# Fourteen more low-part units of a two-block transformer kernel move from VectorE to GpSimd

## The reference, cut to what matters

```python
h    = rmsnorm(x, pre_norm_mix) * (1 + scale_m) + shift_m
q_lat, kv_lat, k_idx, w_idx, z, xbc, dt_raw, g_a, g_b = split(h @ w_in)
qn    = rmsnorm(q_lat, q_norm)
q     = qn @ w_uq                      # 16 heads x 128
q_idx = qn @ w_qidx                    # 16 index heads x 64
rel    = relu(einsum('bqhd,bsd->bqhs', q_idx, k_idx))
iscore = einsum('bqh,bqhs->bqs', w_idx * scale, rel)      # sum over the index heads
iscore = where(key_chunk <= query_chunk, iscore, -inf)
_, idx = top_k(iscore, 64)
logits = q . kv[idx] * scale + bias(position distance);   probs = softmax(logits)
o      = (probs . kv[idx]) @ w_uv @ w_o_attn
y_b    = ssd_mixer(z, xbc, dt_raw, ...) @ w_o_ssd
```

## Time and profile before

| | us |
|---|---|
| median of three executions | 973.84 |
| the profiled execution's own time | 973.98 |
| its span | 972.0 |
| PE busy | 946.3 (97%) |
| DVE busy | 669.4 (69%) |
| ACT busy | 544.4 (56%) |
| POOL busy | 242.2 (25%) |

### The profile page before, as it was taken

The page is one execution under the profiler, slowest core; times in us unless marked ns, Lnnn a source line. Parts: engine busy times, 40 slices in busy tenths (PEclk is TensorE's granted clock), DMA queues, the critical chain, the costliest instruction groups (busy, mean ns, idle before and its releaser), DMA issues.

```text
span 972.0 us, 16471 instructions
## 1 busy us (share of the span) xinstructions
PE 946.3 (97%) x6121; PEld 829.3 (85%) x6121; DVE 669.4 (69%) x1094; ACT 544.4 (56%) x956; POOL 242.2 (25%) x239
## 2 busy tenths in 40 slices
PE   9999999999999999999999999999999999999997
PEld 8987777888877798899989999998889778888786
DVE  5765567777785668975668666677985767755453
ACT  6667666444443666834547455557863754544443
POOL 5205002111122231299932143330230021000100
PEclk9999999999999999999999999999999999999999
DMA  9755347789987713760139756653246677656561
GB/s 293 217 161 190 94 147 231 229 276 289 284 274 257 247 51 97 208 174 22 34 102 311 236 165 183 172 144 88 75 147 213 219 237 242 211 175 192 194 221 66
DMA packets 141594, 179.04 MB, mean 184 GB/s; under 512 B 8124, under 2 KB 117390, under 8 KB 141520
## 3 DMA queue, kind: packets, MB, share of 16 engines
q1 hardware_dynamic: 130624, 144.53, 47.6%
q0 software_dynamic: 10304, 33.18, 11.5%
q10 hardware_dynamic: 592, 0.34, 0.1%
HBM read 176.90 MB, written 1.12 MB: 183 GB/s over the span
## 4 chain that ended last, share of the span: by engine, by line
PE 80%; DVE 8%; ACT 6%; DMA 3%; issue 2%; SPq 0%; DVEq 0%; ACTq 0%
PE bank L1932 26%; PE bank L2021 12%; PE bank L2023 11%; PE bank L2022 11%; DVE w_lo L1333 3%; ACT w_hi L869 2%; PE bank L2191 1%; PE bank L2454 1%; PE bank L1963 1%; PE bank L2450 1%; PE bank L2477 1%; DMA w_raw<-in_w_in 1%; PE bank L2385 1%; PE bank L2073 1%; DMA w_raw<-in_w_down 1%
## 5 line engine op out<-in xcount | busy, mean ns | idle before, releaser
L1333 DVE TENSOR_TENSOR w_lo<-w_raw,w_hi 128x1024 fp32r<-128x1024 f32 (+1 forms) x239 | 286.0, 1221 | 91.2 <-ACT w_hi L869 86.8
L869 ACT ACTIVATE w_hi<-w_raw 128x1024 fp32r<-128x1024 f32 (+1 forms) x258 | 262.1, 1037 | 117.7 <-PE bank L2023 50.6
L1932 PE MATMUL bank<-h_hi,w_hi 128*128 128x256 f32 x560 | 162.9, 291 | 1.9 <-DVE w_lo L1333 1.0
L1932 PE MATMUL bank<-h_lo,w_hi 128*128 128x256 f32 x560 | 158.3, 283 | 0.0
L1932 PE MATMUL bank<-h_hi,w_lo 128*128 128x256 f32 x560 | 158.2, 282 | 0.0
L2021 PE MATMUL bank<-w_hi,h_hi 128*128 128x512 f32 x384 | 152.1, 396 | 1.9 <-DVE h_lo L1333 1.9
L2023 PE MATMUL bank<-w_hi,h_lo 128*128 128x512 f32 x384 | 150.3, 391 | 0.0
L2022 PE MATMUL bank<-w_lo,h_hi 128*128 128x512 f32 x384 | 150.1, 391 | 0.0
L1932 PEld LDWEIGHTS bank<-h_hi,w_hi 128*128 128x128 f32 x560 | 107.2, 191 | 3.4 <-DVE w_lo L1333 2.0
L1932 PEld LDWEIGHTS bank<-h_lo,w_hi 128*128 128x128 f32 x560 | 107.3, 192 | 0.0
L1932 PEld LDWEIGHTS bank<-h_hi,w_lo 128*128 128x128 f32 x560 | 107.1, 191 | 0.0
(11 more groups left out here) (463 smaller groups left out, 1810.3 us busy)
## 6 DMA issues: line engine op xcount, KB each, us to landing
w_raw<-in_w_in SPq DMA_DIRECT2D x84, 512.0 KB, 3.8
ada_raw<-in_ada_w POOLq DMA_DIRECT2D x48, 512.0 KB, 6.0
w_raw<-in_w_gate_up SPq DMA_DIRECT2D x88, 256.0 KB, 5.4
w_raw<-in_w_ffn_in SPq DMA_DIRECT2D x88, 256.0 KB, 4.0
w_raw<-in_w_down SPq DMA_DIRECT2D x22, 512.0 KB, 6.5
w_raw<-in_w_ffn_out SPq DMA_DIRECT2D x22, 512.0 KB, 4.5
w_raw<-in_w_out SPq DMA_DIRECT2D x16, 512.0 KB, 4.0
w_raw<-in_w_o_ssd SPq DMA_DIRECT2D x16, 512.0 KB, 3.4
```

What stands on the lines that cost most here:

```text
L869: act.activation(high(u, n), w_raw[:, u % RING, 0:n], ACT.Copy).then_inc(hi_ready, 1)
L1333: return dve.tensor_tensor(dst, src, hi.bitcast(F32), ALU.subtract)
L1932: ins = pe.matmul(out_b[:, s, :], w[:, kk, c], x[:, k0 + k, :], start=k == 0 and s == 0 and step == 0, stop=k == sum(st.ks) - 1 and s == 1 ...
```

## The change

POOL makes the low parts of the eight `w_uq` units, of all ten `z` units and of the first two `s_z2` units, twenty in all where it made six; it does so ahead of its wait for the index sums, of the DMA of `w_uv` and of `reached`. DVE makes none from the first `w_uq` unit to the second unit of `s_z2`: its two low parts ahead of the rounds, the one in each round, the three before the top-k and the two behind the mask go.

```diff
-    pool_topk = range(s_z.u0 + 4, s_z2.u0)
+    pool_topk = range(s_uq.u0, s_z2.u0 + 2)
...
         pool.affine_select(out=pick[:, :], in_=pick[:, :], pattern=[[-1, 16 * P]], compare_op=ALU.is_ge,
                            fill=0.0, base=15, channel_multiplier=16).then_inc(pick_ready, 1)
+        for u in range(s_uq.u0, s_z.u0):
+            split(u)
+        for u in range(s_z.u0, s_z2.u0 + 2):
+            split(u)
         pool.wait_ge(ix_sum, 8)
         pool.dma_start(w_uv[:, :, :], a["w_uv_2"].rearrange("h c d -> c h d")).then_inc(uv_in, 16)
-        for u in pool_topk:
-            split(u)
...
-        split_to(s_uq.u0 + 2)
         for r in range(8):
...
             ins.then_inc(ix_sum, 1)
-            split_to(min(s_uq.u0 + r + 3, s_z.u0 + 1))
             dve.wait_ge(ix_sum, r + 1)
         link(dve.tensor_tensor(isc[:, :, :], isc[:, :, :], shut[:, :, :], ALU.add))
-        split_to(s_z.u0 + 4)
...
         dve.tensor_tensor(mask[:, :, :], isc[:, :, :], shut[:, :, :], ALU.add).then_inc(mask_ready, 1)
-        split_to(s_z2.u0 + AHEAD)
+        split_to(s_z2.u0)
```

## The result

The changed kernel takes 979.84 us in the median (978.83 to 981.28, four runs) against 973.23 (972.25 to 973.98): the ratio is 1.0068, 95% interval 1.0056 to 1.0081. It is slower by 6.6 us where 3.8 were forecast. The direction was right; the time is 2.2 us above the forecast of 977.6 and 0.2 us above the upper end of the range, 979.6.

The account below looks back on a forecast made before the run. PE was taken to bound the kernel, so time is won only where PE stands still. Lead -1.7, wait +4.0 and clock +1.5 gave +3.8 us: 977.8 on the profiled execution, forecast 977.6 us, range 975.2 to 979.6.

Parts of the forecast that it names:

- The three holes: PE's idle waits before the first `w_uq` unit (1.15 us), z0 (0.40) and z1 (0.91): 2.46 us, all the change can win.
- the lead s: PE's lead over the old timetable from the filled holes, after held sums: taken as 1.7 us.
- The shared port: DVE operations with two SBUF inputs wait for the running POOL instruction; index sums fall behind by 0.53 us a round.
- the mask, held twice: DVE's mask behind the top-k, delayed by two POOL splits, is there by 427.6.
- the dearer port: Rival: POOL gets between the sums more often, s about 0, wait 4.0 us, with the clock +5.5: 979.3; chance 0.14.
- The queue on POOL: Two `s_z2` splits, `w_uv` DMA and `reached` end at 432.0 - s; PE waits 4.0 us before the first logits tile.
- its three signs of being wrong: First logits bracket under 2 us, the mask and not `reached` ending it, or PE reaching z1 later than 401.8.
- The clock: PE's 4.0 us gap before the logits halves its clock for about 3.4 us, costing 1.5 us.
- The sum: Over the profiled execution: -1.7 + 4.0 + 1.5 = +3.8 us.
- The faster case: Rival: POOL isn't late at the end of `z`, so the holes are simply filled: -2.1, 971.7 us; chance 0.05.

Follow-up runs that it names:

- e3_halves: The changed kernel with each of POOL's twenty splits issued as two instructions on half the columns: 979.18 us, ratio 1.0051 to the kernel before.
- e2_only_z2: The kernel before with only the first two `s_z2` units given to POOL, the `w_uv` DMA behind them: 979.04 us, ratio 1.0052.
- e4_only_uq: The kernel before with only the eight `w_uq` units given to POOL: 974.94 us, ratio 1.001.
- e5_both: The changed kernel with two `s_z2` units back on DVE and POOL's `w_uq` and z0 to z3 splits halved: 971.57 us, ratio 0.9984 to the kernel before.
- e6_first_two: The kernel before with only the first two `w_uq` units given to POOL: 971.66 us, ratio 0.9982.
- e1: The changed kernel with only the first two `s_z2` units back on DVE behind the mask: 980.9 us, ratio 1.0073 to the kernel before.
- e7_z1: The kernel before with only unit z1 given to POOL: 972.85 us, ratio 0.9997.
- v3_four: The kernel before with the first two `w_uq` units, z0 and z1 given to POOL, and z2 on DVE between the last two rounds' sums: 971.23 us, ratio 0.9984.
- the last four experiments: e5_both, e6_first_two, e7_z1 and v3_four, which share one set of runs of the kernel before (median 973.65 us).

## Why the prediction was wrong, step by step

- **The three holes, and the lead s.** Right in kind. The first went whole (1.15 us). The lead at z1 was 2.23 - 0.88 = 1.35 us, forecast 1.7. z0 had to wait 0.92 for POOL (1.1 us by the starts) instead of 0.4. ReLU 5 already waited 0.66 us for the held sums of round 3, one round earlier than I had it, so the copy of z0 came later, and its split took 2.63 us instead of 2.4.
- **The shared port.** The mechanism was read rightly from the earlier trace rows and shown by e3_halves. Its size is the step that failed: "each further two-input step letting one POOL split past, the top-k starts at about 407 at the latest, ends at 422.8, and the mask, held twice, is there by 427.6." The top-k started at 413.67 and the mask came at 430.84. I had let one split past per step only behind the sums, 5 us in all, and let the sums themselves "end near 402". But POOL makes z0 to z3 just while DVE does the last two rounds, and then z4 to z6; with splits of 2.5 us queued back to back, each sum sits one out. Seven steps from 394.29 on, six sums and the addition, cost 2.5 to 2.8 us instead of 0.5 to 0.7, some 14 us more together. "POOL has one split a round and then waits for ACT", my reason against the dearer port, held only as long as the splits were those of `w_uq`. The miss on the sums (they ended at 410.8, not 402) was larger than the one on the mask: I had taken the mask as held twice, but POOL was through with its splits at 426.50 and nothing behind the top-k was held (0.62 and 0.77 us), which gave 3.4 us back by luck.
- **The queue on POOL.** Right: 4.0 us forecast, 4.04 measured where it stands alone (e2_only_z2). In the changed kernel `reached` came near 429.7, as the sum in the prediction has it (431.9 less 2.2), but the mask came a good microsecond later, at 430.84, and set the wait, 5.2 us. The prediction named the mask as what is late next, and of its three signs of being wrong ("if the mask and not `reached` ends it") this one came true.
- **The clock.** Its fall was forecast, its price was too low. Half speed lasted 6.8 us and not 3.4, in the changed kernel and in e2_only_z2, where PE had stood still for 5.2 and 4.0 us; after the 1.89 us gap of e4_only_uq it lasted 3.4. From the first logits tile to the third PE lost 2.5 us, forecast 1.5. I took the only example in the trace as the price for any gap. Why it lasts twice as long here was not tested.
- **The sum.** -1.35 + 5.1 + 2.5 + 0.6 = 6.9 against -1.7 + 4.0 + 1.5 = 3.8; the profiled spans show 6.0, as 0.9 came off in the first block by chance. The 0.6 has no term in the prediction and no cause shown here. The direction was not luck, since the queue on POOL alone gives it (e2_only_z2).
- **Rivals.** The dearer port (979.3) was nearest, with a chance of 0.14. Its place, the sums, was right, and it says that the top-k and the mask slip too, but its number comes from s = 0, from PE held up in the rounds, and its wait is still the 4.0 us of `reached`. The port acted at the other end, through the mask, with s at 1.35; that 979.3 lies so near is in part luck. The faster case was far off as long as both late ends stood; e5_both shows that it was two edits away.

## What to carry to other kernels

Work given to a helper engine whose instructions hold up a chain of short dependent ones is to be priced, while the helper's queue is full, by the length of its instruction times the number of links, not by the sum of the work: 0.49 us became 2.5 here, and halving the instruction gave 7 us back. Such work is best put beside operations that it doesn't hold up (here the 16 max and match-replace pairs, which kept their pace with POOL busy nearly all the time), and not in front of something that the critical engine waits for next. When two engines feed the same wait, work out both arrival times to the end; mending one alone shows nothing (980.9 and 979.2), both together 971.6 (e5_both).

## What else the runs showed of the hardware

The clock of PE falls in the first block in some executions and in others not, with the same program there. In the execution of before it fell behind the 1.88 us gap. In that of the changed kernel it didn't, behind the same gap:

```profile
126.00:132.00 6.00, 5.58 (x25) 4.65 (x26) 4.35 (x6) 2.79 (x4) 0.00 (x0) 1.00 0.42 119
```

In e6_first_two (and e1, e4 and e7) it fell earlier, with PE busy all through the stretch, 3.4 us at half speed in eight:

```profile
100.00:108.00 8.00, 8.00 (x53) 7.31 (x54) 2.69 (x5) 0.33 (x2) 0.00 (x0) 0.79 0.20 66
```

In e2 it fell near 128, behind the same gap, and in e3, e5 and v3 in neither place. That is 1.5 us or so from one execution to the next, about the spread of a kernel's runs (972.25 to 973.98), and the reason why single profiled spans here are compared only after taking off what differs ahead of the changed stage. What decides whether it falls wasn't tried.

It also blurs the medians of the last four experiments. Of the 33 executions of the kernel before, the 16 with a mean granted clock of 0.999 or more have a median of 972.60 us and the other 17 of 974.33. Executions at 0.999 or more alone, sorted so only after the fact, give 971.38 for e5_both, 971.22 for e6_first_two, 971.87 for e7_z1 and 970.93 for v3_four: 1.2, 1.4, 0.7 and 1.7 us less than before. The traces, from the first index product to the first logits tile, show 1.5, 1.1, 0.7 and 1.8. So e7_z1 most likely does win a little, and v3_four most likely wins most.

The DMA that POOL issues for `w_uv` took its 1.24 us on POOL's queue wherever it stood, and a POOL split of 512 columns took 1.27 to 1.57 us beside DVE's sums. I put the up to 0.3 us down to the sum that was running as the split was released; that wasn't tested by itself.
